# One level of Strassen's method in the last 16 chunks of an FFN's up projection

## The chip, the cores and the metric

The kernel runs on one core of a Trainium2 chip. The metric is the device time of one execution in microseconds; the time given for a kernel is the median of its runs. All inputs and results are fp32.

## The reference, cut to what matters

Two transformer blocks on 512 tokens of width 1024: a first block with a stick-breaking and a forgetting attention, a second with a pooling, an RWKV and a differential mixer, then a cross attention to 256 memory rows, then a feed-forward part (FFN) of width 2816. The change concerns the last:

```
def conv_ffn(xn, w_up, conv_w, conv_b, w_down):     # xn = rmsnorm(x, ffn_norm_g)
    h = xn @ w_up                                   # 512x1024 @ 1024x5632
    a, b = jnp.split(h, 2, axis=-1)
    rhs = conv_w.reshape(CONV_W, 1, D_FF).astype(a.dtype)
    c = lax.conv_general_dilated(a, rhs, ...) + conv_b      # three taps along the tokens
    return (jax.nn.gelu(c, approximate=False) * b) @ w_down
```

## The kernel before

Everything is kept transposed: features lie on the 128 partitions, tokens along the columns, so the normed input of the FFN is `KD` = 8 tiles of 128x512 and the hidden width is `KF` = 22 tiles.

**Products of three.** An fp32 operand is split in two fp32r parts: ScalarE (ACT) copies it to its high part, and GpSimd (POOL) or VectorE (DVE) subtracts this from the raw value and gets the low part. `mm3` (and the inner loop over `k` of the down projection) makes one fp32 product of three matmuls: high by high, high by low, low by high.

**The stream of weights.** SyncE (SP) loads the weights as chunks of 128x2048 fp32 (1 MB) into three raw slots (`RAW`); ACT makes the high parts in one of two slots (`HI`), POOL's `low_weights` makes the low parts over the raw ones in four pieces. A chunk is loaded when the chunk three before it is used, and ACT splits it when the one two before it is used. Each engine works through one list in program order, so whatever an engine waits for also holds what stands behind it on that engine.

**Up projection.** For each of 11 values of `j` two chunks are used: one for two tiles of the half `a`, one for two of `b`. Each tile is 24 matmuls of 512 columns. The input `h` is scaled by the gain but not by the inverse root mean square (`rms`), which DVE multiplies in when it takes a tile out of PSUM. DVE then makes the three taps (`L2413` to `L2415`), ACT the gelu (`L1818`), DVE the product with `b` (`L2433`, `L2435`). Between these DVE also makes sums of quarters of the result (`L2421` to `L2425`) and their low parts (`L1855`) for the next stage.

**Down projection.** It is already done by one level of Strassen's method: seven products (`FORMS`) of quarters or sums of quarters, for each of `DOWN_PAIRS` = 4 pairs of output tiles, so 28 pieces of 33 matmuls of 256 columns. The weights come as pieces of 128x1408 fp32 (704 KB). ACT's `down_high` makes their high parts. POOL makes the low parts of seven of the 28 pieces and of all of the first four (`FROM_POOL`, ten pieces in all), in four groups each; DVE makes the others.

**Sums of the weights.** The four sums of quarters of `w_down` that the seven products need are made during the first block, in DRAM. ACT issues plain copies from DRAM to DRAM (two at `L1367`, one at `L1392`, one at `L1496`), POOL issues DMAs that add to them (`add`, `L2509`, four per sum). The copy at `L1392` stands directly before the loop of the stick-breaking attention.

**That attention.** It runs over 16 steps `i` of head pair and query block. In `stick_step(i)` ACT takes the scores out of PSUM, makes their logarithms (`L1415` to `L1417`), and for `n = i - 1` the weights (`L1423`, semaphore `stick_w`). In step 1 it also issues a small store of the forget gates' sums (`nF_kept`, 16 KB, `L1426`), and in step 4, before the high part of the next chunk, it waits until that store has landed and loads the rows back as a broadcast (`L1429`):

```
                if i == 1:
                    act.wait_ge(sem("nF_ready"), 1)
                    act.dma_start(nF_kept, nF[0:HEADS, :]).then_inc(sem("nF_stored"), 16)
                if i == 4:
                    act.wait_ge(sem("nF_stored"), 16)
                    act.dma_start(nF_bc[0], nF_kept[0:2, :].partition_broadcast(P)).then_inc(sem("nF0_loaded"), 16)
```

TensorE (PE) does, in each step, the scores of `i`, the transposes of the weights of `n = i - 2` (`head_turns`, which waits for `stick_w` to reach `n + 1`), a part of another projection (`side`), and the values of `n = i - 3`.

Of the kernel before, what the change touches and what calls it, by code (L numbers as in the profile page):

```python
# [7 lines left out]
F32 = mybir.dt.float32  # L8
# [5 lines left out]
P = 128  # L14
# [44 lines left out]
STREAM = 85  # L59
# [6 lines left out]
FORMS = 7  # L66
DOWN = FORMS * DOWN_PAIRS
DOWN_RAW, DOWN_HI = 5, 4
GROUPS = ((0, 3), (3, 6), (6, 9), (9, 11))
# [74 lines left out]
def build(nc, x_in, mem_in, params_in, consts_in, ada_in, stream_in, with_f_in, down_in, out, x2_kept, kx_kept, vx_kept, nF_kept, sums_kept):  # L144
    with ExitStack() as ctx:
# [96 lines left out]
        nF_rows = sb("forget_rows", 2, T)  # L242
# [108 lines left out]
        ox_raw = [at(2048, 4, T), at(7200, 4, T)]  # L351
        ox_lo = [at_r("xa_low_a", 2048, 4, T), at_r("xa_low_b", 7200, 4, T)]
# [7 lines left out]
        t_raw = [at(KF * T + quad * i, DOWN_K, DOWN_N) for i in range(2)]  # L360
        t_lo = [at_r(f"t{i}_low", KF * T + quad * i, DOWN_K, DOWN_N) for i in range(2)]
        t_hi = [at_r(f"t{i}_high", KF * T + quad * (2 + i), DOWN_K, DOWN_N) for i in range(2)]

        def quarter(v, half, side):
            return v[:, DOWN_K * half:DOWN_K * (half + 1), DOWN_N * side:DOWN_N * (side + 1)]

        q11, q12, q21, q22 = (quarter(gact_raw, i, n) for i in range(2) for n in range(2))
        form_raw = [q11, t_raw[0], q22, t_raw[1], q12, q11, q21]
        form_lo = [quarter(gact_lo, 0, 0), t_lo[0], quarter(gact_lo, 1, 1), t_lo[1], quarter(gact_lo, 0, 1),
                   quarter(gact_lo, 0, 0), quarter(gact_lo, 1, 0)]  # L370
        conv_in = at(2 * KF * T, 3, T + 2)

# [48 lines left out]

        DOWN_SLOT = [(STREAM + i) % RAW for i in range(RAW)] + [3, 4]
        DOWN_HI_SLOT = [(STREAM + i) % HI for i in range(HI)] + [2, 3]
        FROM_POOL = tuple(i for i in range(DOWN) if i < DOWN_PAIRS or i % DOWN_PAIRS == 0)

# [15 lines left out]
        def down_loaded(i):  # L441
            s, turn = down_slot(i), i // DOWN_RAW
            if s < RAW:
                return loaded[s], 16 * ((STREAM + i % DOWN_RAW - 2) // RAW + 1 + turn)
            return sem(f"first{s - RAW}_loaded"), 16 * (turn + 2)
# [5 lines left out]
        DOWN_BEFORE = {2: 1, 3: 0, 4: 2, 5: 4, 6: 3}  # L451
        DOWN_ONTO = (2, 3, 5)
# [31 lines left out]
        def _(pe):  # L484
# [629 lines left out]
            for j in range(KF // 2):  # L1114
                for half in range(2):
                    slot, w = next_chunk(KD, 256)
                    for mi in range(2):
                        o = M.take(pe, ("up", 2 * j + mi, half))
                        for k in range(KD):
# [4 lines left out]
                            mm3(o, [p_[:, k, P * mi:P * (mi + 1)] for p_ in w], h(k), k == 0, k == KD - 1,  # L1124
# [5 lines left out]
                    chunk_end[-1] = ("up", 2 * j + 1, half)  # L1130
            M.use([4, 5, 6, 7, 0, 1, 2, 3])
            for i in range(DOWN):
                f, p = down_form(i)
                if f in DOWN_BEFORE:
                    pe.wait_ge(sem("down_moved"), DOWN_PAIRS * DOWN_BEFORE[f] + p + 1)
                else:
                    M.take(pe, ("down", f, p))
                o = down_bank(i)
                whi, wlo = (v(i).rearrange("p (k n) -> p k n", k=DOWN_K) for v in (down_hi, down_lo))
                for k in range(DOWN_K):  # L1140
                    g = k // 3
                    if i not in FROM_POOL and k == 0:
                        pe.wait_ge(sem("down_low"), i + 1 - sum(j < i for j in FROM_POOL))
                    elif i in FROM_POOL and k % 3 == 0:
                        pe.wait_ge(sem("down_low_pool"), len(GROUPS) * FROM_POOL.index(i) + g + 1)
                    if p == 0 and f < 2:
                        pe.wait_ge(sem("forms_split"), DOWN_K * f + k + 1)
                    elif p == 0 and k % 3 == 0:
                        pe.wait_ge(sem("forms_split"), 2 * DOWN_K + len(GROUPS) * (f - 2) + g + 1)
# [4 lines left out]
                    mm(o, wlo[:, k, :], right[0], False, last, sem("down_done") if last else None, skip=True)  # L1154
# [4 lines left out]
        def _(act):  # L1159
# [13 lines left out]
            def split_weights(part=0, parts=1):  # L1173
# [5 lines left out]
                if c >= STREAM:  # L1179
                    down_high(c - STREAM)  # L1180
# [13 lines left out]

            def down_high(i):

                act.wait_ge(*down_loaded(i))
                if i < DOWN_HI:
# [1544 lines left out]
```

## Time and profile before

| what | us |
|---|---|
| median of 3 runs | 1288.83 (1288.09 to 1290.25) |
| the profiled execution | 1291.47, of which the span from first to last instruction is 1289.7 |
| busy in the span: PE, DVE, ACT, POOL | 1253.3, 699.2, 568.5, 530.7 |
| mean granted clock of TensorE | 0.997 |

Matmuls overlap, so the time of one in the profile is longer than the distance from one to the next; what counts for the length of a stage is that distance. The same holds, less strongly, for VectorE: an instruction starts a little before the one ahead of it ends in the profile. For a DMA the profile gives the time from its issue to its landing.

### The profile page before, as it was taken

To read this page: it belongs to the slowest core of one execution; us is meant where nothing else is said; L and a number is where in the kernel's file an instruction comes from. 1 tells how busy PE (TensorE), PEld (TensorE's weight loads), DVE (VectorE), ACT (ScalarE), POOL (GpSimd) and SP (SyncE) were. 2 spreads that over 40 slices of the span, in tenths; PEclk is the share of its full clock that TensorE was granted. 3 is DMA by queue.
4 is the path that set the end of the run, shared out by engine and by line. 5 is a ranking of instruction groups with operands and counts; after the bars stand their busy time and mean duration, and the time that the engine had idled before them with its cause. 6 is when DMAs were issued, how large, how long until landed. Compare 5 with 4: busy or idle time off the path is not lost.

```text
span 1289.7 us, 20794 instructions
## 1 busy us (share of the span) xinstructions
PE 1253.3 (97%) x8570; PEld 1019.5 (79%) x8570; DVE 699.2 (54%) x1093; ACT 568.5 (44%) x870; POOL 530.7 (41%) x424
## 2 busy tenths in 40 slices
PE   6999999999999999999998899999999999999999
PEld 5788888866678888767786767788788888888999
DVE  3250004886431266686557657265565665766773
ACT  6541444786665233354544544353422221224452
POOL 6544454322234544534242126331444444546321
PEclk9999999999999999999999999999999999999999
DMA  9836795612115452412220013310222222224554
GB/s 387 348 131 243 248 230 191 163 50 97 51 66 188 122 163 79 181 66 76 69 107 16 3 66 131 135 61 34 99 98 98 81 87 94 99 88 172 166 185 151
DMA packets 24907, 165.05 MB, mean 128 GB/s; under 512 B 2792, under 2 KB 2920, under 8 KB 11504
## 3 DMA queue, kind: packets, MB, share of 16 engines
q1 hardware_dynamic: 20448, 128.15, 27.9%
q10 hardware_dynamic: 2064, 24.07, 5.0%
q0 software_dynamic: 2304, 11.54, 4.5%
q8 instruction: 68, 1.11, 0.3%
q14 instruction: 23, 0.19, 0.0%
HBM read 157.43 MB, written 29.38 MB: 145 GB/s over the span
## 4 chain that ended last, share of the span: by engine, by line
PE 89%; DVE 4%; ACT 3%; POOL 2%; issue 1%; DMA 0%; SPq 0%; DVEq 0%; ACTq 0%
PE banks L488 87%; PE banks L495 2%; DVE arena L1985 1%; POOL h_low L2557 1%; DVE arena L1982 1%; DVE arena L1987 1%; POOL weights_low L2557 1%; DMA arena<-in_mem 0%; ACT weights_high L1192 0%; ACT arena L1238 0%; ACT memory_high L1248 0%; ACT arena L1416 0%; ACT arena L1417 0%; ACT arena L1415 0%; DVE arena L1943 0%
## 5 line engine op out<-in xcount | busy, mean ns | idle before, releaser
L2499 POOL TENSOR_TENSOR weights_low<-weights,weights_high 128x512 fp32r<-128x512 f32 x324 | 433.2, 1367 | 580.5 <-ACT weights_high L1192 580.5
L488 PE MATMUL banks<-h_high_low,weights_high 128*128 128x512 f32 x880 | 358.2, 407 | 1.6 <-ACT arena L1443 1.6
L488 PE MATMUL banks<-h_low,weights_high 128*128 128x512 f32 x880 | 348.9, 397 | 0.0
L488 PE MATMUL banks<-h_high_low,weights_low 128*128 128x512 f32 x880 | 348.8, 396 | 0.0
L1192 ACT ACTIVATE weights_high<-weights 128x2048 fp32r<-128x2048 f32 (+2 forms) x90 | 156.3, 1737 | 243.1 <-PE banks L488 226.0
L488 PEld LDWEIGHTS banks<-h_high_low,weights_high 128*128 128x128 f32 x880 | 166.0, 189 | 46.0 <-issue 5.8
L488 PEld LDWEIGHTS banks<-h_low,weights_high 128*128 128x128 f32 x880 | 166.0, 189 | 41.8 <-issue 3.6
L488 PEld LDWEIGHTS banks<-h_high_low,weights_low 128*128 128x128 f32 x880 | 165.8, 188 | 40.4
L488 PE MATMUL banks<-arena 64*64 64x64 f32 (+6 forms) x1800 | 118.1, 263 | 4.1 <-issue 2.6
L488 PEld LDWEIGHTS banks<-arena 64*64 64x64 f32 (+3 forms) x1800 | 85.9, 148 | 29.9 <-issue 23.2
L1238 ACT ACTIVATE arena<-banks 128x256 f32<-128x256 f32 (+4 forms) x82 | 41.9, 519 | 53.4 <-PE banks L495 35.1
L2411 DVE TENSOR_TENSOR arena<-banks,sums 128x512 f32<-128x512 f32 x22 | 15.2, 692 | 78.1 <-PE banks L488 73.0
L488 PE MATMUL banks<-t_high,weights_low 128*128 128x256 f32 x198 | 55.6, 281 | 0.0
L488 PE MATMUL banks<-weights_high,h_high_low 128*128 128x256 f32 (+1 forms) x192 | 55.3, 288 | 0.3 <-ACT arena L1238 0.3
L488 PE MATMUL banks<-weights_high,h_low 128*128 128x256 f32 (+1 forms) x192 | 54.2, 282 | 0.0
L488 PE MATMUL banks<-weights_low,h_high_low 128*128 128x256 f32 (+1 forms) x192 | 54.1, 282 | 0.0
L1221 ACT ACTIVATE sums<-xres 128x512 f32<-128x512 f32 x32 | 20.2, 631 | 70.3 <-DVE xres L2065 39.3
L1938 DVE COPY arena<-banks 128x256 f32<-128x256 f32 (+3 forms) x40 | 25.3, 632 | 47.1 <-PE banks L488 46.2
L488 PE MATMUL banks<-t_high,weights_high 128*128 128x256 f32 x154 | 43.5, 283 | 2.5 <-issue 1.5
L488 PE MATMUL banks<-t_high,h_high_low 128*128 128x256 f32 x154 | 42.7, 277 | 0.0
L2557 POOL TENSOR_TENSOR weights_low<-weights,weights_high 128x384 fp32r<-128x384 f32 (+1 forms) x20 | 21.3, 1094 | 47.3 <-ACT weights_high L1202 47.3
L495 PE MATMUL banks<-consts,arena 128*128 128x128 f32 x245 | 37.2, 277 | 1.6 <-DVE arena L2222 0.8
(360 smaller groups left out, 2371.9 us busy)
## 6 DMA issues: line engine op xcount, KB each, us to landing
weights<-in_stream SPq DMA_DIRECT2D x82, 1024.0 KB, 4.8
sums_kept<-in_down POOLq DMA_DIRECT2D x16, 704.0 KB, 12.8
arena<-in_ada SPq DMA_DIRECT2D x8, 1024.0 KB, 11.9
weights<-in_down SPq DMA_DIRECT2D x9, 704.0 KB, 4.1
weights<-sums_kept SPq DMA_DIRECT2D x9, 704.0 KB, 4.0
sums_kept<-in_down ACTq DMA_DIRECT2D x2, 2816.0 KB, 21.4
sums_kept<-sums_kept ACTq DMA_DIRECT2D x2, 2816.0 KB, 12.6
h<-sums_kept SPq DMA_DIRECT2D x7, 704.0 KB, 4.2
```

The source lines that it names most:

```text
L488: ins = nc.tensor.matmul(o, lhsT, rhs, start=start, stop=stop, skip_group_check=skip)
L495: ins = nc.tensor.transpose(o, i, ident[0:rows, 0:rows])
L1192: nc.scalar.activation(hi_of(c)[:, cols], raw_of(c)[:, cols], ACT.Copy)\
L1221: nc.scalar.activation(SQ[n][i % 2][:, 0:width], src[:, k, 0:width], ACT.Square)\
L1238: nc.scalar.activation(dst, s_, ACT.Copy).then_inc(ring_.out(key), 1)
L1938: nc.vector.tensor_copy(dst, o if src is None else src(o)).then_inc(ring_.out(key), 1)
L1982: link(stt(w, o[:, :, 0:end], 0.0, w, ALU.max, ALU.add))
L1985: ins = nc.vector.tensor_tensor_scan(v, ones(end), v, 0.0, ALU.mult, ALU.add)
L1987: tt(w, o[:, :, 0:end], w, ALU.subtract).then_inc(M2.out(("a", i)), 1)
L2411: tt(a[:, 2:T + 2], o, rms[:, :], ALU.mult).then_inc(M.out(("up", m, 0)), 1)
L2499: nc.gpsimd.tensor_tensor(lo_of(c)[:, cols], raw_of(c)[:, cols], hi_of(c)[:, cols].bitcast(F32), ALU.subtract).then_inc(sem("weights_split ...
L2557: nc.gpsimd.tensor_tensor(down_lo(i)[:, cols], down_raw(i)[:, cols], down_hi(i)[:, cols].bitcast(F32), ALU.subtract).then_inc(sem("down_lo ...
```

## The change

Of the 11 values of `j` of the up projection the first three (`UP_PLAIN`) stay as they were. The other eight, 16 chunks, become 16 "chunks" `c` of Strassen's method, 7 pieces each (`UP_N` = 112 pieces), a piece being 12 matmuls of 256 columns. Even `c` are tiles of `a`, odd ones of `b`. The order of the pieces runs over two chunks, and three of the seven products are added in PSUM onto an earlier one, after that was copied out:

```
+UP_PLAIN = 3
+UP = 2 * (KF // 2 - UP_PLAIN)
-STREAM = 85
+STREAM = 63 + 2 * UP_PLAIN
+UP_STEPS = [[(c, f) for c, fs in ((i, (P1, R5)), (i - 1, (Q4, P3)), (i, (R7, P6, P2))) if 0 <= c < UP for f in fs]
+            for i in range(UP + 1)]
+PAIR_RAW, PAIR_HI = 6, 4
+PAIRS_POOL = []
+PAIRS_DVE = list(range(UP_PAIRS))
-        FROM_POOL = tuple(i for i in range(DOWN) if i < DOWN_PAIRS or i % DOWN_PAIRS == 0)
+        FROM_POOL = tuple(i for i in range(DOWN) if i % DOWN_PAIRS == 0)
```

TensorE:

```
+            for n, (c, f) in enumerate(UP_SEQ):
+                if f == P6:
+                    pe.wait_ge(sem("up_copied"), 2 * c + 1)
+                elif f == Q4:
+                    pe.wait_ge(sem("product_moved"), moved_at(c, SUM3))
+                elif f == P3:
+                    pe.wait_ge(sem("product_moved"), moved_at(c, C22))
...
+                for k in range(KH):
+                    mm(o, whi[:, k, :], right[0], k == 0 and f not in (P6, Q4, P3), False, skip=True)
+                    mm(o, whi[:, k, :], right[1], False, False, skip=True)
+                    mm(o, wlo[:, k, :], right[0], False, last, sem("product_done") if last else None, skip=True)
```

SyncE loads a piece as 128x512 fp32 (256 KB, rows of 2 KB), two for a pair. ACT makes the high part of a pair of pieces in one instruction, VectorE the low part:

```
+            for n, (c, f) in enumerate(UP_SEQ):
+                q = n // 2
+                if n % 2 == 0:
...
+                        sp.wait_ge(sem("product_done"), 2 * (q - PAIR_RAW) + 2)
+                sp.dma_start(piece_of(pair_raw, n), up_from[f][c]).then_inc(pair_loaded(q)[0], 16)
...
+            def pair_high(q):
...
+                    act.wait_ge(sem("product_done"), 2 * (q - PAIR_HI) + 2)
+                nc.scalar.activation(pair_hi(q), pair_raw(q), ACT.Copy).then_inc(sem("piece_hi"), 1)
...
+            def low_pair(q):
...
+                    low(pair_lo(q), pair_raw(q), pair_hi(q), sem("piece_low"))
```

The input of the Strassen part is normed beforehand (8 instructions of VectorE), and its four sums of quarters (128x1024 each), seven high parts (ACT) and seven low parts (VectorE) are made during the three plain `j`. What ACT and VectorE do per chunk: two products are copied out by ACT (`keep`), five quarters by VectorE, the first tap goes to ACT (`tap`), and no tile is multiplied by `rms` any more:

```
+                if f == P2:
+                    moved_(tt(to_tile(c, 0, 0), up_bank(c, P2), k1, ALU.add))
+                    dve.wait_ge(sem("up_copied"), 2 * c + 2)
+                    moved_(tt(k3, up_bank(c, R7), k2, ALU.subtract))
+                    dve.wait_ge(sem("product_moved"), moved_at(c, SUM3))
+                    moved_(tt(to_tile(c, 1, 1), k3, up_bank(c, R5), ALU.subtract))
+                elif f == Q4:
+                    moved_(tt(to_tile(c, 1, 0), up_bank(c, Q4), k2, ALU.subtract))
+                else:
+                    moved_(tt(to_tile(c, 0, 1), up_bank(c, P3), k2, ALU.add))
```

The down projection keeps its seven products and their order. Its sums of quarters are now made inside it, a form ahead of their use, in the memory of the quarters themselves, and the low parts of its pieces 1 to 3 go from POOL to VectorE.

The four sums of quarters of the 16 chunks of `w_up` (4 MB each) are made in DRAM too, by the same two kinds of DMA in between the others. `sums_copied` and `sums_added` count both, so the waits change:

```
             act.wait_ge(sem("sums_added"), 2 * 16 * DOWN_PAIRS)
             act.dma_start(sums_kept[S2], sums_kept[S1]).then_inc(sem("sums_copied"), 16)
+            for to in (S1, S3):
+                act.dma_start(up_sums[to], up_in[A21]).then_inc(sem("sums_copied"), 16)
...
-            act.wait_ge(sem("sums_added"), 3 * 16 * DOWN_PAIRS)
+            act.wait_ge(sem("sums_added"), 5 * 16 * DOWN_PAIRS)
             act.dma_start(sums_kept[S4], sums_kept[S2]).then_inc(sem("sums_copied"), 16)
+            act.dma_start(up_sums[S2], up_sums[S1]).then_inc(sem("sums_copied"), 16)
...
             split_weights()
+            act.wait_ge(sem("sums_added"), 7 * 16 * DOWN_PAIRS)
+            act.dma_start(up_sums[S4], up_sums[S2]).then_inc(sem("sums_copied"), 16)
...
             low_weights(vb - 2, vb + 3)
-            add(S2, A11, 3)
-            low_weights(vb + 3, go)
-            add(S4, A12, 4)
-            low_weights(go, mixers + HI)
+            add(S2, A11, 5)
+            add(S1, A22, 5, True)
+            low_weights(vb + 3, vb + 4)
+            add(S3, A11, 5, True)
+            low_weights(vb + 4, go)
+            add(S4, A12, 7)
+            low_weights(go, go + 1)
+            add(S2, A11, 7, True)
+            low_weights(go + 1, mixers + HI)
...
+            low_weights(mixers + HI, core - 6)
+            add(S4, A12, 8, True)
+            low_weights(core - 6, core)
```

## Rows read from the trace of the kernel before

**Rows 1.** The page, part 4: the chain that ended last, shares by engine.
```profile
PE 89%; DVE 4%; ACT 3%; POOL 2%; issue 1%; DMA 0%; SPq 0%; DVEq 0%; ACTq 0%
```
**Rows 2.** Windows (busy us and instructions per engine) of up, first forms of down, rest.
```profile
926.20:1174.40 248.20, 248.20 (x1060) 199.21 (x1059) 156.69 (x186) 64.00 (x69) 119.80 (x91) 1.00 0.26 91
1174.40:1196.40 22.00, 19.58 (x161) 18.95 (x159) 14.54 (x15) 13.01 (x13) 20.11 (x16) 1.00 0.66 231
1196.40:1286.80 90.40, 90.34 (x765) 90.13 (x765) 55.12 (x65) 38.24 (x36) 19.45 (x20) 1.00 0.53 173
```
**Rows 3.** Timeline of VectorE, up projection: start, us, instruction, idle before it.
```profile
1067.96 0.69 DVE L2411 TENSOR_TENSOR arena<-banks,sums 128x512 f32<-128x512 f32 x1 [4.93 <-PE banks L488]
...
1090.46 0.69 DVE L2411 TENSOR_TENSOR arena<-banks,sums 128x512 f32<-128x512 f32 x1 [4.94 <-PE banks L488]
```
**Rows 4.** Groups by form, up projection: busy us, mean ns.
```profile
L2421 DVE TENSOR_TENSOR arena<-arena 128x256 f32<-128x256 f32 x11 | 16.6, 1512 | 0.0
```
**Rows 5.** Timeline of VectorE with POOL idle: two taps of up; three of down.
```profile
1069.70 0.75 DVE L2414 SCALAR_TENSOR_TENSOR arena<-arena,params 128x512 f32<-128x512 f32 x1
1070.49 0.75 DVE L2415 SCALAR_TENSOR_TENSOR arena<-arena,params 128x512 f32<-128x512 f32 x1
...
1206.58 0.41 DVE L2441 TENSOR_TENSOR xres<-xres,banks 128x256 f32<-128x256 f32 x1
1206.90 1.62 DVE L1855 TENSOR_TENSOR weights_low<-weights,h_high_low 128x1408 fp32r<-128x1408 f32 x1
1208.44 0.69 DVE L1855 TENSOR_TENSOR gact_low<-arena,t_high 128x512 fp32r<-128x512 f32 x1
```
**Rows 6.** The page, part 6: DMA issues, KB each, us to landing.
```profile
out<-xres SPq DMA_DIRECT2D x8, 256.0 KB, 2.7
```
**Rows 7.** Timelines of ACT and POOL, down projection.
```profile
1174.79 1.38 ACT L1202 ACTIVATE weights_high<-weights 128x1408 fp32r<-128x1408 f32 x1 [7.08 <-PE banks L488]
...
1198.98 3.64 POOL L2557 TENSOR_TENSOR h_low<-h,weights_high 128x384 fp32r<-128x384 f32 x4 [2.58 <-ACT weights_high L1202]
```
**Rows 8.** Timeline of ACT and its DMA queue, steps 0 to 5 of the attention.
```profile
213.36 0.48 ACTq L1392 DMA_DIRECT2D sums_kept<-sums_kept  x1
...
220.00 0.53 ACTq L1426 DMA_DIRECT2D nF_kept<-arena  x1
...
233.52 0.34 ACTq L1429 DMA_DIRECT2D forget_rows<-nF_kept  x1
234.48 1.04 ACT L1192 ACTIVATE weights_high<-weights 128x1024 fp32r<-128x1024 f32 x1
...
237.24 0.40 ACT L1423 ACTIVATE arena<-arena 128x256 f32<-128x256 f32 x1
```
**Rows 9.** DMA landings: ACT's queue from 119.85 us (second line L1367), then L1392.
```profile
kx_kept<-arena ACTq DMA_DIRECT2D x1, 1024.0 KB, 8.8
...
DMA to landing us min/median/max: 16.9/21.4/25.9
...
sums_kept<-sums_kept ACTq DMA_DIRECT2D x1, 2816.0 KB, 13.1
```
**Rows 10.** Packets, MB, share of ACT's queue (q10) in 137:143 and 216:220.
```profile
q10 hardware_dynamic: 42, 1.89, 92.6%
...
q10 hardware_dynamic: 30, 1.35, 94.2%
```
**Rows 11.** Timeline of PE in step 6: transposes for step 4's weights.
```profile
241.02 0.39 PE L495 MATMUL banks<-consts,arena 128*128 128x128 f32 x2
```
**Rows 12.** Timeline of PE, then windows: an idle time and the clock (1.00 full) behind.
```profile
551.24 3.34 PE L488 MATMUL banks<-arena,params 64*128 64x512 f32 x6 [2.91 <-issue]
...
552.00:554.00 2.00, 2.00 (x5) 0.84 (x3) 1.91 (x3) 1.39 (x3) 0.00 (x0) 0.51 0.03 8
554.00:556.00 2.00, 2.00 (x6) 1.33 (x5) 1.93 (x4) 1.94 (x4) 0.00 (x0) 0.64 0.00 0
```
**Rows 13.** Timeline of POOL: the issue of the third sum's adds.
```profile
241.52 3.32 POOL L2509 DMA_DIRECT2D sums_kept<-in_down  x4
```

More of the change, by code:

```diff
@@ L443, in down_loaded @@
             if s < RAW:
-                return loaded[s], 16 * ((STREAM + i % DOWN_RAW - 2) // RAW + 1 + turn)
+                return loaded[s], 16 * (sum(c % RAW == s for c in range(2, STREAM)) + turn + 1)
             return sem(f"first{s - RAW}_loaded"), 16 * (turn + 2)
@@ L1819, in _, with gelu, first_high_of @@
-            assert chunks[0] == STREAM + HI
-            for i in range(HI, DOWN):
+            def gelu(m):
+                act.wait_ge(sem("conv"), m + 1)
+                nc.scalar.activation(gact_raw[:, m, :], gact_raw[:, m, :], ACT.Gelu).then_inc(sem("gelu"), 1)
+            def first_high_of(m):
+                if m < DOWN_K:
+                    if m < 2 * UP_PLAIN:
+                        M.wait_out(act, ("up", m, 1))
+                    else:
+                        act.wait_ge(sem("forms_made"), made_at("gact", m))
+                    high(t_hi[0][:, m, :], q11[:, m, :], sem("forms_hi"))
@@ new lines, in _ @@
+            split_weights()
+            for m in range(2):
+                gelu(m)
+            split_weights()
+            for i, f in enumerate(T_ORDER):
+                act.wait_ge(sem("token_made"), KD + 4)
+                high(th_hi[f], th_raw[f], sem("token_hi"))
+            split_weights()
+            for m in range(2):
+                first_high_of(m)
+            for m in range(2, 4):
+                gelu(m)
+            split_weights()
+            for m in range(2, 4):
+                first_high_of(m)
@@ new lines, in _, with form_high @@
+            for _ in range(HI):
+                split_weights()
+            assert chunks[0] == STREAM + HI
+            def form_high(f):
+                act.wait_ge(sem("product_done"), UP_N + DOWN_PAIRS * (f - 1))
+                for g, (first, last) in enumerate(GROUPS):
+                    act.wait_ge(sem("forms_made"), {R5: made_at("T1", DOWN_K - 1), P6: made_at("T2", g), R7: made_at("T3", g),
+                                                    Q4: made_at("T4", g)}.get(f, made_at("gact", KF - 1)))
+                    high(t_hi[f % 2][:, first:last, :], form_raw[f][:, first:last, :], sem("forms_hi"))
@@ L1821, in _ @@
+            for i in range(3):
+                down_high(i)
+            form_high(R5)
+            for i in range(3, DOWN):
                 down_high(i)
@@ new lines, in gact_out @@
+            def gact_out(c):
+                for half in range(2):
+                    m = up_tile(c, half)
+                    dve.wait_ge(sem("gelu"), m + 1)
+                    if half == 0:
+                        dve.wait_ge(sem("product_moved"), moved_at(c, C12))
+                    tt(gact_raw[:, m, :], gact_raw[:, m, :], other[:, half, :], ALU.mult).then_inc(sem("forms_made"), 1)
+                    if m >= DOWN_K:
+                        first_form(m)
+            for m in range(2):
+                conv(m, True)
@@ L2697, in lay_stream @@
         parts.append(lay_chunks(np.asarray(a[key])[0], 256))
-    halves = [lay_chunks(up[:, FFN * i:FFN * (i + 1)], 256) for i in range(2)]
+    halves = [lay_chunks(up[:, FFN * i:FFN * i + 256 * UP_PLAIN], 256) for i in range(2)]
     parts.append(np.stack(halves, 1).reshape(2 * halves[0].shape[0], P, -1))
```

429 lines of the change are left out of this document (304 added, 125 removed).

## The prediction, made before the changed kernel was run

> **What bounds the kernel now.** First the chain of work that ended last: 89% of it is TensorE [rows 1], so a matmul that goes gives back its time, and another engine counts only where PE comes to wait for it. Next the stages of the FFN by windows [rows 2]. The reader is to see that PE is busy all 248.2 us of the up projection, at the full clock, that VectorE is busy 157 us of them and POOL 120 (nearly all of it low parts), and that the down projection is as dense but for its start: 22.0 us for 159 matmuls (the 924 less the 765 of the third window). Then, for each thing that the change adds elsewhere, the timeline of the engine or queue it is put on: this is where I find the other half of the answer, in the attention of the first block, 700 us ahead of the matmuls that are saved.
>
> **What goes: matmuls.** The first tile of one `j` is taken out at 1067.96 us and that of the next at 1090.46 [rows 3]: 22.50 us for 96 matmuls of 512 columns, 0.2344 each. Eight `j` are 180.0 us. In their place come 16 x 7 x 12 = 1344 matmuls of 256 columns. The down projection shows their price: 765 in 90.40 us with no gap worth the name [rows 2], 0.1182 each, so 158.8 us. Gain: **21.2 us**, which is the eighth that one level of Strassen's method saves, less 1.3 us.
>
> The Trainium skill speaks against narrower matmuls ("TensorE: Matmul & The Clock Gate", the passage on sustained spacing): it gives some 81 ns for 128 columns and 131 for 512, so that half the width would cost far more than half the time. By a line between its two figures 256 columns would cost about three quarters of 512, an estimate from that page, and the change would lose some 56 us. The trace disagrees in these fp32r products, where 256 columns cost 0.504 of 512 [rows 2, 3], and I go by the trace.
>
> **Does anything hold PE in the Strassen part?** A piece is 12 x 0.1182 = 1.42 us, a chunk 9.93. VectorE's price per instruction, from start to start with POOL idle [rows 5]: 128x256 0.32, 128x1408 1.54 (so 1.13 for the 1024 of a pair), 128x512 0.61 by the same slope, a tap behind another 0.79. Per chunk on average: 3.5 low parts of pairs 3.96, five quarters out 1.6 and 0.1 for the one that waits for its neighbour, two taps 1.58, one product with `b` 0.61, one small form or low part 0.32: 8.2 us, 82% of 9.93. In order, an odd step (four pairs) fills its 9.9 us nearly to the end and an even one (three) has about half a microsecond left. What PE waits for soonest is `SUM3`: due 2.84 us after the end of P2, made 0.9 us after it if VectorE is free then. So VectorE may be late by 1.9 us before PE feels it. Today's 1.51 us for a 128x256 [rows 4] comes from POOL's subtractions beside it, and POOL has nothing to do in this stage any more. ACT has 3.5 x 1.04 for the pairs (1024 columns, at 234.48 [rows 8]), some 3 for copies, taps and gelu: 7 of 9.9. The pairs are loaded ten pieces (14.2 us) ahead of PE and four (5.7) ahead of ACT; 256 KB in rows of 2 KB landed in 2.7 us as a store [rows 6], two behind each other should take 3 to 4. I put **1 us** for small waits over the whole part; bounds 0 and 6.4 (0.4 us a chunk, if VectorE's instructions had their full durations and each wait cost 0.1).
>
> Preparing the input (8 scalings, 4 sums, 7 high parts, 7 low parts: about 18 us of VectorE and 7 of ACT) lies in the three plain `j`, 67 us in which VectorE has about 25 of its own. Even with POOL in its way the bank of a `b` tile is needed 17 us after its product is done. Nothing.
>
> **The seam to the down projection.** Before, PE lost 22.0 - 159 x 0.1182 = 3.2 us there [rows 2], to low parts. Now: P2 of the last chunk ends, PE has two pieces left (2.8 us); VectorE needs 1.2 for three quarters and 1.6 for the taps, ACT 0.65 for the gelu, then 1.38 for the high part of piece 0 and POOL 0.9 for its first quarter [rows 7]: 6.1, so PE stands 3.3 us. The same as before. The first form's pieces then cover VectorE, which now has their low parts and four groups of two forms: about 14 us of work in 15.6. I put **0.5 us**; bounds 0 and 3.
>
> **What is added ahead: DMAs.** The sixteen new adds take POOL 3.3 us for four [rows 13]. Behind each of them POOL next waits for a high part of ACT, mostly for longer than that; behind the third, where eight follow each other and wait for the copies below, the next low part comes only after PE has gone on again. Nothing.
>
> The copies are another matter. ACT issues a 2.88 MB copy at 213.36 us; now two of 4.19 MB follow on the same queue. Then in step 1 (220.0) it puts the 16 KB store of the forget gates on that queue, and in step 4 it stands at the wait for that store. Today it goes past at or before 233.5 [rows 8], since the copy landed 13.1 us after its issue [rows 9]. Does the store queue behind the copies? From 119.85 us ACT issued a 1 MB store and two copies of 2.88 MB, all within 1.5 us. They landed after 8.8, 16.9 and 25.9 us [rows 9]. Two equal copies that shared the engines would land together; these land one after the other. So a DMA on ACT's queue waits for what is ahead of it.
>
> When does the store land then? Copies moved 1.35 MB in 4 us, 0.338 MB/us [rows 10]. At this rate the 2.88 MB take 8.5 us, so 4.6 of the 13.1 were start and tail. All three: 11.27 / 0.338 = 33.4, and 4.6, from 213.4: 251.4, the store about 1 us later, 252.4. From the wait to the weights of step 4 ACT took 233.52 to 237.64 [rows 8], 4.1 us: now they come at 256.5. PE needed them at 241.02 [rows 11]; `side`, which could fill the gap, stands behind the transposes in PE's order. So PE stands **15.5 us**. In this stage PE has no idle time in which it could win that back. By the same arithmetic at 0.315 MB/us (1.89 MB in 6 us [rows 10]) it is 17.9.
>
> The clock comes on top. After 2.91 us of idling it was 0.51 for 2 us and 0.64 for 2 [rows 12], that is the 1.2 GHz level for most of them: 1.0 + 0.7 = **1.7 us** lost. I take that; bounds 0 (PE's small matmuls here may wait for ACT anyway) and 3.
>
> The other two groups of copies have no such wait behind them: at 390 us ACT's next DMA is 120 us away, near 540 the queue is also free for long. Chunk loads get little of the engines beside a copy, but each has about 19 us until PE would notice, and 7.1 MB take 21 and the tail.
>
> **The sum.** -21.2 + 1 + 0.5 + 15.5 + 1.7 = -2.5 us. The profiled execution took 1291.47, 1.8 more than its span; 1289.0 after. It lies 2.6 above the median of the runs shown, so for the median I forecast 1286.3, rounded **1286**. Most of a real gain is spent at a wait that has nothing to do with it.
>
> **Rivals.**
> *The store does not queue* (or the copies run much faster than I think). For it: the trace has no small DMA behind a large one on this queue, and the store is 8 rows, which need not use the engines that are late. Against it: the landings in rows 9. Then PE loses nothing there: -21.2 + 1.5, to 1269 (1267 to 1273). Chance 0.20. The Trainium skill's "DMA: Bandwidth & Descriptors", section "Queues, rings and completion order", says that each DMA engine takes the descriptors of one ring in their order, which speaks for queueing; it also says that completion is not strictly in order over engines. No row here shows the small case.
>
> *The copies are slower, so the change loses.* The next chunk's load, issued at 213.8, has to share with them, and ACT needs it right behind the wait. The lone copy made 2.88 MB in 13.1 us, 0.22 MB/us all in [rows 9]; if that is the rate for all, the store lands at 265, PE stands 28 us and the time is 1299. It decides from 0.314 MB/us: there the landing is at 255 and gain and loss are equal; slower by 0.2% it is from about 257.6 (0.29 MB/us). For it: that row, and the sharing with accumulating transfers and loads. Against: 0.338 beside a chunk load, and no less than 0.315 while copies were queued behind each other [rows 10]. Chance 0.13.
>
> *VectorE is the bound in the Strassen part.* At 82% with waits in a fixed order it may fall behind by 0.4 us or more a chunk: 6 us and more on top, 1292 to 1300. For it: four pairs in the odd steps. Against: three in the even ones and the 1.9 us of play. Chance 0.07.
>
> **Chances.** The forecast as it stands has 0.60, its own range 1282 to 1290. What can be told from no change here is 0.2%, 2.6 us: 1286.3 to 1291.4. Of the forecast's 0.60 some 0.36 lie below, 0.22 within, 0.02 above; the first rival is wholly faster, the second and third slower but for 0.02. Faster 0.56, same 0.24, slower 0.20. The range must take in the first rival's centre and part of the slow ones: 1267 to 1294.
>
> **What would show it.** Right: a wait of ACT of about 18 us behind `L1423` of step 4 near 234 us, PE idle about 15 us from 241 with a clock near 0.5 behind it; everything until the FFN later by 17; the up projection 21 us shorter than 248.2, PE busy throughout. Wrong: no idle time near 241 (first rival, a gain of 20); idle times of PE inside the Strassen part with VectorE as the releaser (third); a landing after 257 (second). A seam much longer than 3 us would be a term that I undersized.

## The result, and the profile of the changed kernel

The changed kernel takes **1297.71 us** (median of 5 runs, 1295.02 to 1298.71) against 1288.92 (1288.09 to 1290.25) for the kernel before in the same runs: a ratio of 1.0062, 95% interval 1.0048 to 1.0076. It is slower by 0.6%, where 1286 and a range of 1267 to 1294 were forecast. The profiled execution took 1295.86 us, span 1294.0, mean clock 0.991; before it was 1291.47. So between the two profiled executions the loss is 4.4 us, between the medians 8.8: the one of before lies 2.6 above its median, that of after 1.9 below. From the issue of the fourth sum's copy (390 or 411 us) to the first matmul of the up projection the eleven profiles of this document take 531.0 to 536.7 us, though PE's work there is the same: short idle times lie in this stretch, and in some executions a lower clock follows them. A difference of that size there is not explained here.

The chain that ended last, shares by engine, then by line. Against [rows 1] PE falls from 89% to 83%, and one DMA of 16 KB has 3% of the whole time:

```profile
PE 83%; DVE 8%; ACT 4%; DMA 3%; issue 2%; ACTq 0%; POOL 0%; SPq 0%; DVEq 0%
PE banks L571 81%; DMA nF_kept<-arena 3%; PE banks L578 2%; DVE arena L2175 1%; DVE h L2671 1%; DVE h_low L2045 1%; DVE token_sum_low L2045 1%; DVE arena L2177 1%; DVE arena L2172 1%; ACT weights_high L1304 0%; DMA arena<-in_mem 0%; ACT arena L1358 0%; DVE second_low L2045 0%; DVE arena L2612 0%; DMA weights<-in_down 0%
```

**The FFN.** Windows of the three plain `j`, the Strassen part with the seam, and the down projection (busy us and instructions of PE, PEld, DVE, ACT, POOL, then clock, DMA share, GB/s), to stand beside [rows 2]:

```profile
945.30:1016.60 71.30, 68.62 (x292) 54.29 (x291) 63.68 (x63) 26.69 (x29) 37.15 (x23) 1.00 0.27 89
1016.60:1179.20 162.60, 159.59 (x1345) 159.18 (x1343) 135.09 (x203) 91.32 (x127) 1.42 (x2) 1.00 0.58 180
1179.20:1291.20 112.00, 109.84 (x924) 109.09 (x924) 84.64 (x92) 51.61 (x50) 34.99 (x27) 1.00 0.53 182
```

The records of the up matmuls end at 1177.05, so the Strassen part proper is 160.4 us (159.8 were forecast) and the seam 2.2. From the first up matmul on, the FFN takes 345.9 us, before 360.5: the method gives 14.6 us, not the 19.7 of the sum (21.2 less 1 and 0.5). The plain `j` take 71.3 us, and 68.4 before. Their idle times of PE, then what POOL does at the second:

```profile
980.39 0.50 PE L571 MATMUL banks<-ffn_high,weights_high 128*128 128x512 f32 x1 [0.45 <-DVE arena L2614]
...
1005.28 0.50 PE L571 MATMUL banks<-ffn_high,weights_high 128*128 128x512 f32 x1 [2.23 <-DVE arena L2614]
```
```profile
986.56 17.39 POOL L2793 TENSOR_TENSOR weights_low<-weights,weights_high 128x512 fp32r<-128x512 f32 x8 [7.50 <-ACT weights_high L1304]
```

**The attention.** Timeline of ACT and its DMA queue, as in [rows 8]; the bracket is the idle time ahead of an instruction and what ended it:

```profile
213.59 0.48 ACTq L1512 DMA_DIRECT2D sums_kept<-sums_kept  x1
214.10 1.26 ACTq L1514 DMA_DIRECT2D up_sums<-in_up  x2
...
220.24 0.53 ACTq L1548 DMA_DIRECT2D nF_kept<-arena  x1
...
253.82 0.35 ACTq L1551 DMA_DIRECT2D forget_rows<-nF_kept  x1
254.30 1.06 ACT L1304 ACTIVATE weights_high<-weights 128x1024 fp32r<-128x1024 f32 x1 [19.49 <-DMA nF_kept<-arena]
```

ACT stands at the store from 234.8 to 253.8. Its queue (q10: packets, MB, share) and that of the chunk loads (q1) in 222:228 and in 234:240, as in [rows 10]:

```profile
q10 hardware_dynamic: 47, 1.72, 74.8%
q1 hardware_dynamic: 48, 0.39, 21.7%
```
```profile
q10 hardware_dynamic: 46, 1.97, 92.8%
q1 hardware_dynamic: 48, 0.26, 14.2%
```

ACT's queue moved 0.29 and 0.33 MB/us, where I had taken 0.338 throughout. The timeline of PE at the place of [rows 11], and windows of the clock behind it:

```profile
257.52 0.69 PE L578 MATMUL banks<-consts,arena 128*128 128x128 f32 x2 [16.10 <-ACT arena L1545]
258.95 0.58 PE L571 MATMUL banks<-weights_high,h_high_low 128*128 128x256 f32 x1 [0.74 <-ACT arena L1358]
```
```profile
257.00:259.00 2.00, 0.74 (x3) 0.34 (x3) 1.70 (x3) 2.00 (x5) 1.44 (x2) 0.50 0.02 6
259.00:261.00 2.00, 2.00 (x9) 2.00 (x10) 1.97 (x3) 1.94 (x3) 2.00 (x2) 0.50 0.00 0
261.00:263.00 2.00, 2.00 (x11) 1.86 (x9) 1.88 (x4) 0.87 (x2) 2.00 (x5) 0.54 0.24 28
263.00:265.00 2.00, 2.00 (x21) 1.16 (x20) 1.97 (x3) 0.00 (x0) 2.00 (x5) 1.00 0.93 175
```

The clock is 0.50, the 1.2 GHz level, from PE's return at 257.5 until about 263, 5.5 us of which PE idled 0.7: 2.4 us more. Two marks measure the whole: the copy at 213.4 (before) or 213.6, and the issue of the fourth sum's copy at 390.1 or 411.2, 176.7 and 197.6 us apart. **The block costs 20.9 us**: 16.8 of idling, 2.4 at half clock behind it, and 1.7 in 324:330, where behind an idle time of 1.59 us that the kernel before has too the clock is 0.72 here and 1.00 there. 17.2 was forecast; from 19.7 saved it had to stay under that to win.

### The profile page after: what moved, and what is told of

It reads as the page before. It is cut to its first block, busy times and chain, and to the rows that moved or that the text cites. A ratio compares the mean times of both kernels' runs of the same rounds, so it can differ in the third digit from the quotient of the medians.

```text
span 1294.0 us, 22195 instructions
## 1 busy us (share of the span) xinstructions
PE 1236.3 (96%) x9146; PEld 1036.8 (80%) x9146; DVE 763.1 (59%) x1182; ACT 623.0 (48%) x958; POOL 457.6 (35%) x364
## 4 chain that ended last, share of the span: by engine, by line
PE 83%; DVE 8%; ACT 4%; DMA 3%; issue 2%; ACTq 0%; POOL 0%; SPq 0%; DVEq 0%
PE banks L571 81%; DMA nF_kept<-arena 3%; PE banks L578 2%; DVE arena L2175 1%; DVE h L2671 1%; DVE h_low L2045 1%; DVE token_sum_low L2045 1%; DVE arena L2177 1%; DVE arena L2172 1%; ACT weights_high L1304 0%; DMA arena<-in_mem 0%; ACT arena L1358 0%; DVE second_low L2045 0%; DVE arena L2612 0%; DMA weights<-in_down 0%
## 5 line engine op out<-in xcount | busy, mean ns | idle before, releaser
L2793 POOL TENSOR_TENSOR weights_low<-weights,weights_high 128x512 fp32r<-128x512 f32 (+1 forms) x260 | 355.2, 1398 | 491.5 <-ACT weights_high L1304 491.5
L571 PE MATMUL banks<-h_high_low,weights_high 128*128 128x512 f32 (+1 forms) x784 | 290.7, 371 | 1.6 <-ACT arena L1565 1.6
L571 PE MATMUL banks<-h_low,weights_high 128*128 128x512 f32 (+1 forms) x784 | 281.7, 359 | 0.0
L571 PE MATMUL banks<-h_high_low,weights_low 128*128 128x512 f32 (+1 forms) x784 | 281.6, 359 | 0.0
L1304 ACT ACTIVATE weights_high<-weights 128x2048 fp32r<-128x2048 f32 (+2 forms) x74 | 125.7, 1698 | 125.1 <-PE banks L571 87.0
L2045 DVE TENSOR_TENSOR weights_low<-weights,weights_high 128x1024 fp32r<-128x1024 f32 (+1 forms) x61 | 76.8, 1263 | 10.6 <-ACT weights_high L1316 7.4
L1316 ACT ACTIVATE weights_high<-weights 128x1024 fp32r<-128x1024 f32 x56 | 59.0, 1057 | 36.6 <-PE banks L571 35.5
L571 PE MATMUL banks<-token_sum_high,weights_high 128*128 128x256 f32 x192 | 54.0, 281 | 0.8 <-DVE sums L2649 0.8
L571 PE MATMUL banks<-token_sum_high,weights_low 128*128 128x256 f32 x192 | 54.2, 282 | 0.0
L571 PE MATMUL banks<-token_sum_low,weights_high 128*128 128x256 f32 x192 | 54.1, 282 | 0.0
```

The costliest lines, as they stand in the source:

```text
L571: ins = nc.tensor.matmul(o, lhsT, rhs, start=start, stop=stop, skip_group_check=skip)
L1304: nc.scalar.activation(hi_of(c)[:, cols], raw_of(c)[:, cols], ACT.Copy)\
L1316: nc.scalar.activation(pair_hi(q), pair_raw(q), ACT.Copy).then_inc(sem("piece_hi"), 1)
L2045: return tt(lo, raw, hi.bitcast(F32), ALU.subtract).then_inc(done, 1)
L2793: nc.gpsimd.tensor_tensor(lo_of(c)[:, cols], raw_of(c)[:, cols], hi_of(c)[:, cols].bitcast(F32), ALU.subtract).then_inc(sem("weights_split ...
```

## The experiments

Ratios are to the kernel before, run beside each on the same chip; "fell" and "rose" are against the kernel that each is built on.

**1. The two copies behind the store.** They are issued in step 4, after the store was waited for, with a semaphore of their own; the adds move behind them.

```
-            for to in (S1, S3):
-                act.dma_start(up_sums[to], up_in[A21]).then_inc(sem("sums_copied"), 16)
...
                     act.dma_start(nF_bc[0], nF_kept[0:2, :].partition_broadcast(P)).then_inc(sem("nF0_loaded"), 16)
+                    for to in (S1, S3):
+                        act.dma_start(up_sums[to], up_in[A21]).then_inc(sem("up_sums_copied"), 16)
```

> The two 4 MB copies of the up projection's sums are issued in step 4, behind the store of the forget gates' sums and the loading back, instead of ahead of step 0; the adds on them move one and one chunk later. Same work, same DMAs. Theory A (the wait for the store behind the copies costs the 19 us): ACT passes the wait near 234 us as in the kernel before, PE has no idle time near 241, the up projection starts at 926 to 928 us instead of 945.3, and the time falls by 17 to 19 us against the changed kernel, to about 0.992 of the kernel before. Rival B (the 12 MB of copies and adds cost time wherever they run, by keeping the engines from the stream of weights): PE waits elsewhere, the start of the up projection stays above 938 us and the time falls by less than 8 us.

**1276.07 us** (1273.03 to 1278.46), ratio 0.9894 (0.9874 to 0.9915): 21.6 us under the changed kernel. ACT and its queue:

```profile
220.34 0.53 ACTq L1546 DMA_DIRECT2D nF_kept<-arena  x1
233.86 0.34 ACTq L1549 DMA_DIRECT2D forget_rows<-nF_kept  x1
234.24 1.17 ACTq L1551 DMA_DIRECT2D up_sums<-in_up  x2
```

ACT passes the store at 233.9 as before, PE doesn't stand at 241, and the two marks are 176.8 us apart. The same bytes by the same engine, 20 us later, cost nothing.

**2. The store on another queue.** The copies stay; POOL issues the 16 KB store.

```
-                    act.dma_start(nF_kept, nF[0:HEADS, :]).then_inc(sem("nF_stored"), 16)
...
+            pool.wait_ge(sem("nF_ready"), 1)
+            pool.dma_start(nF_kept, nF[0:HEADS, :]).then_inc(sem("nF_stored"), 16)
```

> The copies stay where the change puts them; only the 16 KB store of the forget gates' sums goes from ACT's queue to POOL's. Theory A (it waits for its turn in its own queue): it lands at once, and ACT then waits only for the load of the next chunk, which landed at 240.1 us in the changed kernel; PE idles about 3 us at 241 instead of 16.1 and the time falls by 13 to 17 us. Rival C (the copies take the DMA engines, and any small transfer is late on any queue): ACT stands until 250 us or later as now, and the time falls by less than 4 us.

**1281.51 us** (1280.15 to 1285.75), ratio 0.9927 (0.9908 to 0.9946). So queueing behind the copies was 16 of the 21.6 us. The other 5 are a second wait, which the first had covered: the two marks are 181.6 us apart, 4.8 more than in kernel 1, of which 2.9 are PE's idling below and most of the rest is a clock of 0.72 in 246:252. Timelines of ACT and of PE, then the landings of SyncE's chunk loads issued between 210 and 235 us:

```profile
240.83 1.06 ACT L1304 ACTIVATE weights_high<-weights 128x1024 fp32r<-128x1024 f32 x1 [5.24 <-DMA weights<-in_stream]
```
```profile
244.06 0.44 PE L578 MATMUL banks<-consts,arena 128*128 128x128 f32 x2 [1.86 <-ACT arena L1545]
245.48 0.39 PE L571 MATMUL banks<-weights_high,h_high_low 128*128 128x256 f32 x1 [0.99 <-ACT arena L1358]
```
```profile
DMA to landing us min/median/max: 25.6/25.8/25.9
```

A chunk of 1 MB, which takes 4.9 us in the median of the program, takes 25.8 beside the copies. The prediction gave each load "about 19 us until PE would notice".

**3. The kernel before, with two copies more.** No Strassen in the up projection: two 4 MB copies to a tensor that nobody reads, at the same place.

```
             act.dma_start(sums_kept[S2], sums_kept[S1]).then_inc(sem("sums_copied"), 16)
+            for to in range(2):
+                act.dma_start(extra[to], stream_in[0:4]).then_inc(sem("extra_copied"), 16)
```

> The kernel before with nothing of the change but two copies of 4 MB (of other data, to a tensor that nobody reads) at the place where the change issues its own. Theory A: the whole loss ahead of the FFN comes with these: ACT waits about 19.5 us behind step 4's weights, PE idles 16 us at 241, the clock stays at half for 5 us, the up projection starts at 945 us, and the time rises by 18 to 20 us, 1.015 of the kernel before. Rival B (adds and the changed waits for sums carry part of it): it rises by clearly less, say 10.

**1310.43 us** (1307.90 to 1312.54), ratio 1.0148 (1.0125 to 1.0170): 19 us slower. ACT, then PE:

```profile
253.92 0.35 ACTq L1431 DMA_DIRECT2D forget_rows<-nF_kept  x1
254.39 1.06 ACT L1192 ACTIVATE weights_high<-weights 128x1024 fp32r<-128x1024 f32 x1 [20.29 <-DMA nF_kept<-arena]
```
```profile
257.61 0.69 PE L495 MATMUL banks<-consts,arena 128*128 128x128 f32 x2 [16.91 <-ACT arena L1425]
```

The marks are 197.7 us apart, as in the changed kernel. The whole loss ahead of 411 us is these two copies; the adds to the new sums have no share in it.

**4. Kernel 1 with the gated products first.** VectorE forms the products that free `b` banks ahead of the token sums and between their low parts.

```
+            for m in range(2):
+                gact_plain(m)
             dve.wait_ge(sem("token_made"), KD)
...
                 low(th_lo[f], th_raw[f], th_hi[f], sem("token_split"))
+                if i in (2, 4):
+                    gact_plain(i // 2 + 1)
```

> As the run with the copies behind the store, and in the three plain values of j VectorE makes the products with b ahead of the sums of the input's quarters, and between its low parts instead of behind all seven. Theory D (PE's 2.7 us of idle time there come from two banks held too long, since VectorE's low parts of 1024 columns take 2.24 us each beside POOL's): both idle times go and the time falls by 2.5 to 3 us more, if nothing after it is late. Rival E (VectorE is short of time in that stage altogether, and any order only moves the wait): less than 1 us, with a wait for VectorE at the start of the Strassen part instead.

**1274.37 us** (1272.55 to 1276.51), ratio 0.9873 (0.9850 to 0.9895): fell 1.7, which the intervals don't tell from nothing, and which lies between D's 2.5 and E's 1. In the profile the plain stage is shorter, 69.9 us for 71.3: the wait of 2.7 for `L2614` is gone, and 1.1 for POOL's low parts has come (a row of the waits of PE: total us, times, longest):

```profile
PE banks L571 <- POOL weights_low L2793: 1.1, 2, 0.6
```

**5. Kernel 4 with the first down piece rounded early**, ahead of the last GELU.

```
+                        if i == UP and f == P3:
+                            down_high(0)
                         if f == (Q4 if i < UP else P3):
                             gelu(up_tile(i - 2, 1))
...
-            for i in range(3):
+            for i in range(1, 3):
                 down_high(i)
```

> Built on the kernel with later copies and the products first (1274.4 us, 0.987 of before), with one step moved: ScalarE rounds the high part of the first down piece ahead of the last GELU instead of behind it, so that GpSimd can make its low parts before Strassen's last product ends. Theory A (the seam's idle time is this order): in the changed kernel TensorE stands 2.2 us at 1177.1 us, where the rounding ran at 1176.35, behind the GELU of 1175.81; it falls to under 0.7 us, and the time to 1272.3 us (1271.5 to 1273.0), 0.9857 of before. Theory B (the seam is bound by VectorE's chain from the last products to the gated activations, the low parts of the second form and the forms behind it): the idle time turns up again as waits for VectorE within the next 15 us of the down projection, and the time stays within 0.7 us of 1274.4. I hold A at 0.45.

**1275.65 us** (1274.22 to 1278.67), ratio 0.9904 (0.9884 to 0.9924): no gain, as B had it, though 1.3 above kernel 4 where B allowed 0.7; the intervals overlap. PE's waits from the seam on, kernel 5:

```profile
1158.91 0.36 PE L571 MATMUL banks<-t_high,weights_high 128*128 128x256 f32 x1 [0.90 <-DVE weights_low L2047]
1174.49 0.36 PE L571 MATMUL banks<-t_high,weights_high 128*128 128x256 f32 x1 [1.64 <-DVE second_low L2047]
1177.83 0.55 PE L571 MATMUL banks<-t_high,weights_high 128*128 128x256 f32 x1 [2.04 <-DVE second_low L2047]
```

In kernel 4 PE stood 2.21 at the seam and 1.05 for `second_low`. Now the seam's wait is gone and 4.6 us turn up in the next 24 (B had said 15). Behind the last up matmul kernel 5 takes 115.4 us and kernel 4 takes 114.0. From the start of the Strassen part to the end it is 275.9 against 275.5 only because the Strassen part before, with the same waits, ran 1.0 us shorter in this execution. VectorE's chain sets this stretch.

**6. Kernel 4 with every fourth pair by POOL.**

```
-PAIRS_POOL = []
-PAIRS_DVE = list(range(UP_PAIRS))
+PAIRS_POOL = [q for q in range(UP_PAIRS) if q % 4 == 3]
+PAIRS_DVE = [q for q in range(UP_PAIRS) if q % 4 != 3]
```

> Built on the kernel with later copies and the products first (1274.4 us), with the low parts of every fourth pair of the Strassen chunks (14 of 56) made by GpSimd, half a pair at a time, instead of VectorE. Theory A (the two engines slow each other, as beside the low parts of the plain chunks, where VectorE's 128x1024 took 2.24 us instead of 1.14 and GpSimd's 128x512 took 2.17 instead of 1.26): VectorE saves 14 x 1.14 = 16 us and is slowed during 28 x 1.3 to 2.2 = 36 to 62 us of GpSimd's, which costs it 15 to 30 us; its busy time in the Strassen stage goes from 136 us to 135 to 150 and TensorE sees nothing of it or waits some 1 to 3 us more: 1274 to 1277.5 us, expected 1275. Theory B (GpSimd is free help): VectorE's busy time falls to 120 us, the wait of 0.8 us for the last sum goes: 1273.4. I hold A at 0.8.

**1273.63 us** (1271.87 to 1273.95), ratio 0.9876 (0.9859 to 0.9893): no difference. Windows over the first 157.5 us of the Strassen part, kernel 4 and then kernel 6:

```profile
995.35:1152.85 157.50, 157.50 (x1321) 157.31 (x1319) 129.25 (x192) 88.09 (x124) 0.00 (x0) 1.00 0.58 182
```
```profile
993.63:1151.13 157.50, 157.50 (x1321) 157.31 (x1319) 119.81 (x178) 88.28 (x124) 39.88 (x28) 1.00 0.57 182
```

Both theories had a number wrong. VectorE's busy time falls by 9.4 us, not by nothing as A had it; 14 low parts of 1.22 are 17.1, so POOL's help slows the rest by 7.7. The slower ones read both operands from SBUF (a second tap 0.87 us for 0.75, a small form 0.54 for 0.42); those that read a PSUM bank took what they took before. So did VectorE's remaining low parts (1.22): by their start times they hardly ever ran beside POOL's, 0.9 us in all. And the wait of 0.8 for the last sum stays, against B. As VectorE isn't the bound, who makes these parts does not matter.

**7. Kernel 2 with its two copies in packets of 4 KB.** What they had before follows from ACT's queue, lines of the page of kernel 2 and then of kernel 7:

```profile
q10 hardware_dynamic: 2368, 40.83, 8.7%
```
```profile
q10 hardware_dynamic: 4288, 40.83, 8.9%
```

The two copies of 4.19 MB are 2048 packets of 4 KB now; the queue has 1920 more than before, so they were 128 of 64 KB. The "about 17 KB" of the expectation is the mean over the whole queue, and wrong for these copies; nor does a chunk load go in 4 KB: its packets are 8 KB (0.39 MB in 48, above).

```
-                act.dma_start(up_sums[to], up_in[A21]).then_inc(sem("sums_copied"), 16)
+                act.dma_start(up_sums[to], up_in[A21], max_dma_last_dim=4096).then_inc(sem("sums_copied"), 16)
```

> Built on the kernel with the forget rows stored on GpSimd's queue (1281.5 us, 0.9927 of before), with one thing changed: the two 4 MB copies of the up weights go in packets of at most 4 KB, as the chunk loads do, where they went in packets of about 17 KB. Theory A (a chunk load starves because the engines take turns by packet and the copies' packets are four times its own): beside the copies the chunk loads land after some 10 to 15 us instead of 25, ScalarE no longer waits 5.24 us for a chunk at 240 us, the granted clock stays up, and the time falls by 3 to 5 us, to 1277.5 (1276.5 to 1279). Theory B (the share does not hang on the packets): landings stay over 20 us and the time within 1 us of 1281.5. I hold A at 0.6.

**1277.68 us** (1276.28 to 1283.18), ratio 0.9920 (0.9889 to 0.9951); the interval reaches over kernel 2's, so the time alone doesn't decide. The landings do (the same loads as in experiment 2); behind them, what is left of ACT's wait:

```profile
DMA to landing us min/median/max: 10.5/12.7/14.8
```
```profile
240.57 1.06 ACT L1304 ACTIVATE weights_high<-weights 128x1024 fp32r<-128x1024 f32 x1 [3.00 <-issue]
```

12.7 us for 25.8. The wait for the chunk is gone; the 3.00 left are the issue of `forget_rows` on ACT's queue, 3.93 us instead of 0.34. The Trainium skill ("DMA: Bandwidth & Descriptors", section "Queues, rings and completion order") says that a DMA engine takes turns between queues by the packet; these landings agree, with half the time beside packets a sixteenth as large, and so does the changed kernel, where in 234:240 the loads moved 0.26 MB and the copies 1.97, about as 8 KB to 64.

The stage gained next to nothing by it, against A's 3 to 5 us: the two marks are 181.2 us apart, and were 181.6 in kernel 2. The issue of the two copies now takes 5.78 us of ACT's queue instead of 1.26, and ACT stands 4.45 us there and 3.00 at `forget_rows`. The 3.8 us between the medians are not from this stage.

**8. Kernel 1 without POOL beside the tokens' low parts.**

```
                     slot, w = next_chunk(KD, 256)
+                    w = (w[0], w[0]) if j == 2 else w
...
-                        cols = slice(n * i, n * (i + 1))
+                        cols = slice(n * i, n * i + (16 if c in (67, 68) else n))
```

It leaves out nearly all low parts of the last two plain chunks; PE multiplies their high parts twice instead, so its matmuls are as many.

> Built on the kernel with the copies behind the store (1276.1 us, 0.9894 of before). It leaves out nearly all of GpSimd's low parts of the last two plain up chunks (16 of 512 columns in each of 8 pieces), and TensorE multiplies the high parts a second time in their place, so that its matmuls are as many as before. Theory A (the three plain steps lose 2.9 us because GpSimd's 17.4 us of low parts run beside VectorE's seven 128x1024 low parts of the tokens, on a port that they share): those seven take 1.14 us each instead of 2.24, 7.7 us less in all, the wait of 2.3 us for the gated products goes, and the plain steps take 68.4 to 69 us instead of 71.3: 1273.5 us (1273.0 to 1274.5). Theory B (VectorE's time here is its own, 2.24 us being what seven low parts with three operands take beside the normed input): the low parts stay at 2.24 us and the time within 0.8 us of 1276.1. I hold A at 0.85.

**1272.05 us** (1270.80 to 1273.19), ratio 0.9865 (0.9849 to 0.9882): fell 4.0 in the medians, where A had 2.6, with intervals that overlap kernel 1's; in the plain stage of the profile, which decides, it is 2.5. VectorE in the changed kernel, then in kernel 8; distances from start to start are 2.24 and 1.16:

```profile
987.09 2.32 DVE L2045 TENSOR_TENSOR h_low<-h,h_high_low 128x1024 fp32r<-128x1024 f32 x1
989.33 2.31 DVE L2045 TENSOR_TENSOR token_sum_low<-arena,token_sum_high 128x1024 fp32r<-128x1024 f32 x1
```
```profile
965.93 1.24 DVE L2046 TENSOR_TENSOR h_low<-h,h_high_low 128x1024 fp32r<-128x1024 f32 x1
967.09 1.23 DVE L2046 TENSOR_TENSOR token_sum_low<-arena,token_sum_high 128x1024 fp32r<-128x1024 f32 x1
```

The three plain `j` take 68.8 us instead of 71.3; before it was 68.4.

**9. The changed kernel with small packets.** The edit of experiment 7 alone.

> The changed kernel (1297.7 us, 1.0062 of before) with one thing changed: its two 4 MB copies go in packets of at most 4 KB, where they went in some 17 KB; they and the 16 KB store of the forget rows stay where they were on ScalarE's queue. Smaller packets brought the chunk loads beside the copies from 25.6 us to 10.5 where the store was on another queue. Theory A (the store waits for the bytes ahead of it in its queue, whatever the packets): at 234 us ScalarE still waits 18 to 23 us for the store, TensorE stands 14 to 19 us at 241 us, and the time is 1297 us (1294 to 1300). Theory B (the block hangs on the packets, as the chunk loads' delay did): the store lands within 25 us of its issue, ScalarE waits under 12 us, TensorE under 8, and the time falls to 1285 us or lower. I hold A at 0.85.

**1293.45 us** (1290.40 to 1299.26) beside 1286.77 for before, ratio 1.0062 (1.0039 to 1.0085): the changed kernel's ratio, to a digit that is chance. But A's 18 to 23 us at the wait for the store came in another form. ACT's queue, then ACT:

```profile
214.54 5.95 ACTq L1514 DMA_DIRECT2D up_sums<-in_up  x2
...
223.62 12.27 ACTq L1548 DMA_DIRECT2D nF_kept<-arena  x1
```
```profile
235.94 0.60 ACT L1358 ACTIVATE arena<-banks 128x512 f32<-128x512 f32 x1 [11.91 <-issue]
...
256.80 1.06 ACT L1304 ACTIVATE weights_high<-weights 128x1024 fp32r<-128x1024 f32 x1 [4.59 <-DMA nF_kept<-arena]
```

With more packets the queue takes the store only after 12.3 us, and ACT stands there instead; the store lands at 256.3, no sooner. PE stands 11.6 us at 225 and only 2.2 from 259 on; the marks are 196.4 us apart, 1.2 less than in the changed kernel. The store waits for the bytes ahead of it, whatever their packets.

## Why the prediction was wrong

**The mechanism was the right one, the wait for the store behind the copies. One term that was put at nothing cost 2.9 us, and three others were too small: PE's stand, the clock and the seam.** Against the forecast of -2.5 us for the profiled execution stand +4.4: the block is 3.7 larger, the FFN gains 5.1 less (2.9 the preparation, 1.3 the seam, 0.6 the Strassen part), and some 1.9 came back elsewhere, within what executions differ by.

- *Matmuls, 21.2 us less*: right. The Strassen part is 160.4 us with its waits, forecast 159.8. TensorE's 256 columns at 0.118 us held.
- *The copies: "the store about 1 us later, 252.4", "PE stands 15.5 us"*: mis-sized. The store landed by 253.8; PE stood 16.1 and 0.7. Experiments 1, 2, 3 and 9 show that this wait is the order of one queue.
- *The clock, "1.7 us lost"*: mis-sized; 2.4 behind the stand and 1.7 near 325 us. I took the recovery behind 2.91 us of idling [rows 12] for the one behind 16. Experiment 3 measures block and clock together at 21.0.
- *"Preparing the input ... Nothing"*: **the step that failed.** It cost 2.9 us, the largest error of a single term: PE waited 0.45 and 2.23 us for VectorE to free banks (`L2614`). The sum of VectorE's work, some 43 us in 67, hid that it comes in one piece in front of products that free banks, and that POOL makes 17.4 us of low parts beside just these 15.6. I had used POOL's slowing for [rows 4], and weighed it here with one clause ("even with POOL in its way"). Experiment 8 takes the collision away and 2.5 of the 2.9 us with it. By the Trainium skill ("SBUF — State Buffer", section "Who interferes with whom") a VectorE instruction with two SBUF inputs contends with a GpSimd instruction that reads SBUF, by an exclusive lock on what they share; the traces fit: 1.16 us alone and 1.26 for POOL's 128x512 make 2.4 in turns, and 2.24 were measured.
- *Waits in the Strassen part, "1 us"*: right, 0.8 before the last sum and nothing else. VectorE was busy 135 of 162.6 us. Its price for a pair, 1.13 us, was 1.14. That "VectorE alone makes the low parts" costs nothing (experiment 6) and the third rival is dead.
- *The seam, "0.5 us"*: 1.8; behind the last up matmul all takes 114.1 us, before 112.3. PE stood 2.2 instead of 3.3 (its terms add to 5.7 us and not to 6.1, which makes a stand of 2.9), but waits of 2.0 for VectorE's low parts followed, which I had put at 14 us of work in 15.6. POOL's first quarters slow it there too: the first 128x1408 low part took 2.16 us, against 1.62 with POOL idle [rows 5]. Experiment 5 shows that shortening one wait lengthens the other.
- *POOL's adds, and the chunk loads beside the copies, nothing*: the adds right (the marks of experiment 1 are 176.8 us apart, before 176.7). Of the loads the words were wrong and only the sum spared: a wait of 5 us lay hidden inside the longer one.

**The rivals.** The second (slower copies) was nearest in number, 1299 against 1297.7, and not in mechanism: its point of decision was a landing after 257 with PE idle 28 us. The first was refuted: the store does queue. The kernel that it described is experiment 1: ratio 0.9894, 13.7 us under before, where it had 19.8.

The forecast hung on a balance of 21.2 saved and 17.2 lost, and the errors of block, clock, preparation and seam all had one sign. Of the 11.4 us between 1286.3 and the median, 6.9 are these, in the profiled executions. By these alone it would be 1293.2, still inside 1267 to 1294. The other 4.5 lie in how the two profiled executions stand to their medians. The mean clock goes with it (0.991 in the two shortest executions of the changed kernel, 0.989 in the other three), but why it differs stays open.

## What to carry to other kernels

Before a large DRAM-to-DRAM copy goes on a queue, find the next DMA on that queue whose completion somebody waits for, and put the copy behind it: here the same bytes cost 21 us or nothing, by their place alone. Then ask who else loads at that time: beside packets of 64 KB a load in packets of 8 KB took five times its usual time, beside packets of 4 KB half of that. But small packets are no gain by themselves: they filled the queue and held the engine that issues (4.45 and 3.00 us in kernel 7, 11.91 in kernel 9), and in their stage won 0.4 and 1.2 us. Low parts that VectorE makes in a burst should not lie beside GpSimd's: a stage's busy sums don't show such a meeting, the due times of the two do.

## What the hardware showed that I had not expected

- A 1 MB load on SyncE's queue took 25.8 us beside 64 KB packets of ACT's queue and 12.7 beside 4 KB ones (4.9 in the median of the program). A 16 KB store on POOL's queue took 11.6 us beside the large packets, 7.1 beside the small.
- A queue can be full for its issuer: behind copies of 4 KB packets an issue on ACT's queue took 12.27 us, where it takes 0.53 otherwise, and ACT computed nothing meanwhile. Behind the same copies in 64 KB packets it took 0.53.
- The clock stayed at its 1.2 GHz level for 5.5 us after PE's return from 16 us of idling; after 2.91 us of idling it was low for some 4 [rows 12].
